# From block 1 to block 2 of a three-block transformer on one core: the two norms made row block by row block, and their preparations moved

## Chip, cores and metric

One Trainium2 chip, one of its cores. The metric is the time of one execution on the device, in microseconds (us); the kernel is one launch. Engines are named as in the profile: PE (TensorE, with PEld for its weight loads), DVE (VectorE), ACT (ScalarE), POOL (GpSimd) and SP (SyncE, which here issues transfers).

## What is computed

Three different transformer blocks, one after the other, on one sequence of 512 tokens of width 1024, all in float32. Cut to what matters:

```
x = first_block(x, c, ...)     # retention, dilated attention, then 32 experts, top 4; ends with a norm
x = second_block(x, ...)       # begins with a norm, then projections, attention, pooling, feed-forward
return third_block(x, ...)

def rms_norm(x, g):
    return x * rsqrt(mean(x * x) + EPS) * g
# at the turn: x = rms_norm(x, g_final); h = rms_norm(x, attn_norm_g_2); u = h @ w_in_2
```

So at the turn from block 1 to block 2 there are two norms in a row: the first gives the residual stream of block 2, the second, of that, gives the input of its projections. With s the sum of squares of x and s' that of x times the gain, both roots follow from the two sums alone: the second norm's sum is s' + EPS (s + D EPS), up to the factor 1/D.

## The kernel before, in words

Tokens are held as NT = 4 tiles of P = 128 rows; the features are D = 1024, or KD = 8 groups of 128 when turned. Weights come as chunks of 1 MB through a ring of six slots (`RING`), which SP fills in a fixed order; each consumer counts a chunk as used (`chunk_used`), and SP then loads the one six places on. A stage is a `Block`: a piece of program for each engine, with all engines meeting at its end. A function scope (`Kit.scope`, one for each block of the model) ends with another such meeting, in which SP clears semaphores.

**Precise products.** A float32 weight piece is split in two: ACT rounds it (`make_high`, L312) and POOL subtracts (`make_low`, L317). A chunk is split in two halves, places 0 and 1, in the tile `split_w`. The activations are split the same way, in `pair`. A product is three matmuls: high by high, low by high, high by low. `SplitAhead` is what one stage does for the first chunk of the next: `high_ahead` and `low_ahead` make place 0. `Onward` goes further: it makes place 1 too (`high`, `low`) and multiplies place 0 (`products`, L363) before the stage ends, so that the next stage begins with place 1 (L661 in `linear_split`) while ACT and POOL make the next piece.

**The experts' stage** (`mixture`) runs 34 units of work in a loop whose order is written out by hand: ACT rounds (L2149), DVE subtracts (L2159), PE multiplies (L2399 with the high, L2403 with the low part), POOL gathers rows and adds results into memory by indirect transfers (L2310). The low parts live in two buffers, `moe_low0` (two of six halves) and `moe_low1` (four), which is allocated in `mixture`. When the last unit's results are in memory, SP loads the four tiles of x back (L2521), each with its own semaphore `x_arrived[t]`.

**The turn** (`leave_and_enter`, one Block) is where the change is:

- SP issues the loads of columns, of the lambda vectors and of the modulation bias, then makes the tables of relative bias: a row out to memory (L1577, when DVE has copied it), spread (L1580), back in as tables (L1585); `bias.sp_end` waits until these are there.
- ACT issues a few loads (`bias.sp_load`, `C.sp`), rounds place 1 of the next chunk (`onward.high`), loads the square-root table by a one-column root (`act_root_table`, L158), then squares x and x times gain for each tile with the sum in an accumulator (L1231, L1234), takes all roots in one instruction (L1237), makes the sigmoid of the condition vector (`M.act_begin`, L989), the exponential of lambda (`lam.act`, L1637), shares the evacuation of the turned tiles (`N.act_evac`: L910, L926) and makes two tiles of the residual (L1245).
- DVE multiplies the four tiles by the gain (L1254), copies the bias row (L1603) and the columns (L770), does the first lambda operations (`lam.dve_begin`, L1630 to L1633), closes the sums of all tiles at once (L1260, L1263), inverts (L1266), scales the four tiles (L1270), shares the evacuation (`N.dve_evac`: L950, L933), makes the other two residual tiles (L1273), then the condition vector (`M.dve_begin`: L999, L1003) and the last of lambda (`lam.dve_end`: L1642, L1643).
- PE makes the bias row (L1598) and turns the columns (L766), waits for all four tiles (`N.pe_turn`: 32 transposes, group by group of features, L904), then does `onward.products`.
- POOL does only `onward.low`.

The next stage is `linear_split` for `b2_qkv` (L661, then L674), then `rest_projections` (L459), then `diff_attention`, which is the first to read the bias tables.

## Time and profile before

| | |
|---|---|
| three runs, median (lowest to highest) | 3656.51 us (3655.53 to 3659.17) |
| the profiled execution, its own time | 3660.48 us |
| its span | 3658.7 us |
| mean granted clock of TensorE | 0.961 |
| PE busy | 3401.1 us (93%) |
| PEld busy | 2758.6 us (75%) |
| DVE busy | 2094.0 us (57%) |
| ACT busy | 1762.2 us (48%) |
| POOL busy | 1036.4 us (28%) |
| HBM read | 669.00 MB |

The span is cut by the page in 40 slices of 91 us; in the slices of the experts PE and DVE are both at nine tenths or more, and the turn falls in the one after, where PE is at six tenths. Shares of the whole span say little of a turn of some 40 us; it is read from the timeline, from the waits and from windows. A timeline row gives the start, the time taken (of several instructions together where it says xN), the engine, the line, output and input, and in brackets how long the engine was idle before and what ended that. PEq, ACTq and SPq are the queues of an engine. In windows the columns are busy time and count of PE, PEld, DVE, ACT and POOL, then the granted clock as a share of full speed, the busy share of the transfer engines and GB/s.

### The profile page before, as it was taken

The page shows a single profiled execution, that of the slowest core. Times are in us where ns is not written, and L with a number is a line of the kernel's source. Part 1 is how long each engine was busy: PE and PEld are TensorE (multiplying, and loading weights), DVE is VectorE, ACT ScalarE, POOL GpSimd, SP SyncE. Part 2 cuts the span into 40 slices and gives each one's busy share as a digit, 9 for nine tenths or more (in the row PEclk, how much of TensorE's full clock was granted, in tenths as well). Part 3 has the DMA queues.
Part 4 walks back from the last instruction along what each step waited for, and adds up shares of the span by engine and source line. Part 5 has one row for each costly group of instructions (what it writes and reads, how often), then busy time and mean ns, then how long its engine had stood idle before and what let it go on. Part 6 is the DMA issues. An engine that isn't in the chain of part 4 may idle for free. (4 is left out here: it accounts for less than half of the span.)

```text
span 3658.7 us, 55859 instructions
## 1 busy us (share of the span) xinstructions
PE 3401.1 (93%) x20953; PEld 2758.6 (75%) x20953; DVE 2094.0 (57%) x2485; ACT 1762.2 (48%) x2315; POOL 1036.4 (28%) x435
## 2 busy tenths in 40 slices
PE   7989999989999999999999697899999987789997
PEld 4877777668888888888888583678887866678886
DVE  3320121279999999999999426411142155346665
ACT  3222333257777777777777424322233243133333
POOL 2334222212232323232323230134443300034443
PEclk9999999989999999999999899799999988889999
DMA  8213343359999999999999527023232210012321
GB/s 285 77 61 102 119 129 121 112 215 371 378 369 377 368 380 366 382 365 378 367 383 365 184 89 294 21 84 104 87 98 70 93 31 4 7 59 94 102 93 40
DMA packets 245517, 696.92 MB, mean 190 GB/s; under 512 B 17878, under 2 KB 149834, under 8 KB 186748
## 3 DMA queue, kind: packets, MB, share of 16 engines
q1 hardware_dynamic: 235196, 658.52, 48.5%
q0 software_dynamic: 9936, 36.18, 3.8%
q8 instruction: 111, 1.82, 0.2%
q14 instruction: 34, 0.28, 0.0%
q10 hardware_dynamic: 240, 0.12, 0.0%
HBM read 669.00 MB, written 30.23 MB: 191 GB/s over the span
## 5 line engine op out<-in xcount | busy, mean ns | idle before, releaser
L317 POOL TENSOR_TENSOR split_w<-ring,split_w 128x1024 fp32r<-128x1024 f32 (+1 forms) x294 | 698.5, 2376 | 1647.3 <-ACT split_w L312 1468.3
L2159 DVE TENSOR_TENSOR moe_low<-ring,moe_high 128x2048 fp32r<-128x2048 f32 x408 | 929.0, 2284 | 18.4 <-ACT moe_high L2149 17.4
L2149 ACT ACTIVATE moe_high<-ring 128x1024 fp32r<-128x1024 f32 x810 | 827.5, 1058 | 102.9 <-PE psum L2403 102.4
L312 ACT ACTIVATE split_w<-ring 128x1024 fp32r<-128x1024 f32 (+1 forms) x294 | 304.5, 1036 | 1034.5 <-PE psum L488 608.1
L2399 PE MATMUL psum<-moe_high,moe_xe 128*128 128x512 f32 x2176 | 585.3, 391 | 0.0
L2399 PEld LDWEIGHTS psum<-moe_high,moe_xe 128*128 128x128 f32 x2176 | 410.0, 188 | 84.0
L2310 POOL DMA_INDIRECT moe_y_rows<-moe_ye,moe_target x34 | 197.4, 5807 | 696.3 <-DVE moe_ye L2214 696.3
L488 PE MATMUL psum<-pair,split_w 128*128 128x512 f32 x1488 | 339.5, 390 | 4.3 <-PEq L3755 4.3
L2403 PE MATMUL psum<-moe_low,moe_xe 128*128 128x512 f32 x1088 | 336.3, 390 | 0.0
L488 PEld LDWEIGHTS psum<-pair,split_w 128*128 128x128 f32 x1488 | 280.4, 189 | 62.8 <-POOL split_w L317 4.4
L488 PE MATMUL psum<-b_pair,split_w 128*128 128x512 f32 x1392 | 321.9, 392 | 5.8 <-PEq L1388 2.6
L488 PEld LDWEIGHTS psum<-b_pair,split_w 128*128 128x128 f32 x1392 | 262.2, 189 | 63.2 <-issue 8.8
L2399 PE MATMUL psum<-moe_high,moe_aT 128*128 128x512 f32 x1088 | 301.9, 399 | 0.0
L2403 PEld LDWEIGHTS psum<-moe_low,moe_xe 128*128 128x128 f32 x1088 | 204.5, 188 | 43.3
L488 PE MATMUL psum<-b_hpair,split_w 128*128 128x512 f32 x1008 | 228.6, 389 | 0.0
L2399 PEld LDWEIGHTS psum<-moe_high,moe_aT 128*128 128x128 f32 x1088 | 196.8, 188 | 36.3
L488 PEld LDWEIGHTS psum<-b_hpair,split_w 128*128 128x128 f32 x1008 | 189.2, 188 | 39.3
L2403 PE MATMUL psum<-moe_low,moe_aT 128*128 128x512 f32 x544 | 168.0, 390 | 0.0
L674 PE MATMUL psum<-split_w,b_hpair 128*128 128x512 f32 x672 | 156.8, 395 | 7.3 <-DVE b_hpair L565 7.1
L674 PEld LDWEIGHTS psum<-split_w,b_hpair 128*128 128x128 f32 x672 | 127.9, 191 | 35.9 <-issue 9.2
L459 PE MATMUL psum<-split_w,b_pair 128*128 128x256 f32 x1152 | 144.6, 288 | 4.1 <-PEq L727 2.2
L459 PEld LDWEIGHTS psum<-split_w,b_pair 128*128 128x128 f32 x1152 | 142.0, 196 | 7.3 <-issue 4.5
(636 smaller groups left out, 4361.7 us busy)
## 6 DMA issues: line engine op xcount, KB each, us to landing
ring<-in_w_experts SPq DMA_DIRECT2D x408, 1024.0 KB, 8.1
ring<-in_w_mod SPq DMA_DIRECT2D x48, 1024.0 KB, 6.1
ring<-in_w_in SPq DMA_DIRECT2D x39, 1024.0 KB, 5.3
ring<-in_w_up SPq DMA_DIRECT2D x33, 1024.0 KB, 5.1
ring<-in_w_in SPq DMA_DIRECT2D x44, 512.0 KB, 5.2
ring<-in_w_down SPq DMA_DIRECT2D x20, 1024.0 KB, 5.1
ring<-in_w_gate SPq DMA_DIRECT2D x11, 1024.0 KB, 5.3
ring<-in_w_out SPq DMA_DIRECT2D x8, 1024.0 KB, 6.2
```

Of the source, the lines that this page charges most:

```text
L312: self.nc.scalar.activation(high, raw, ACT.Copy).then_inc(self.K.rounded, 1)
L317: self.nc.gpsimd.tensor_tensor(low, raw, high.bitcast(F32), ALU.subtract).then_inc(self.K.split, 1)
L459: ins = self.nc.tensor.matmul(out, x(a, r0 + k), w[:, b, k, :], start=(opens and r0 + k + a + b == 0), stop=(closes and r0 + k == KD - 1 a ...
L488: ins = self.nc.tensor.matmul(out[:, tile, :], w[:, a, k, cols], pair[:, b, r0 + k, :], start=(r0 + k + a + b == 0), stop=(r0 + k == nk - ...
L674: ins = nc.tensor.matmul(out[:, t, 0:width], x[:, a, k, t * P:(t + 1) * P], w[:, b, k, :], start=(r + k + a + b == 0), stop=(r + k == tota ...
L2149: self.nc.scalar.activation(self.B["high"][:, j % HALVES, :], self.raw(j), ACT.Copy).then_inc(self.high, 1)
L2159: self.nc.vector.tensor_tensor(flat(self.low_of(j, 2)), self.K.ring[:, self.ring_slot(j // 2), :], high, ALU.subtract).then_inc(self.low, 2)
L2310: self.nc.gpsimd.indirect_dma_start(self.B["y_rows"], bass.IndirectOffsetOnAxis(ap=self.B["target"][:, 0:1], axis=0), self.B["ye"][:, :], ...
L2399: nc.tensor.matmul(out, lhs[:, part, k0 + k, :], high[:, k, :], start=(k0 + k + part == 0 and not started), stop=False)
L2403: ins = nc.tensor.matmul(out, lhs[:, 0, k0 + k, :], low[:, k, :], start=False, stop=(k0 + k == KD - 1))
```

## The change

At the end of the experts' stage ACT and POOL now make both halves of the next chunk (`high_whole`, `low_whole`), and ACT then takes a one-column root into a new tile `moe_root`, allocated ahead of `moe_low1`. In the turn `onward.high`, `onward.low` and `act_root_table` are gone. Sums, roots, inversions and scalings are done tile by tile. The exponential of lambda and the first lambda operations come after the residual tiles. The transposes are done tile by tile, with matmuls whose results nobody reads (`idle`) ahead of them: 12 of 384 columns ahead of the first tile, eight of 128 columns ahead of each later one, into a bank that is overwritten later. The wait for the bias tables goes from the turn to the start of SP's part of `rest_projections`.

```diff
--- before.py
+++ after.py
@@ -179,6 +179,12 @@
                 sp.wait_ge(self.chunk_used, n + 1)
                 self.issue(sp, n + RING)
 
+    def idle(self, count, out):
+
+        n = out.shape[-1]
+        for _ in range(count):
+            self.nc.tensor.matmul(out, self.w[:, 1, 0, 0:P], self.w[:, 1, 1, 0:n], start=True, stop=True)
+
     def wait_chunk(self, pe, n):
         pe.wait_ge(self.landed[n % RING], self.stream.landed_at[n])
 
@@ -323,6 +329,15 @@
     def low_ahead(self, po):
         if self.next is not None:
             self.make_low(po, self.next, 0)
+
+    def high_whole(self, sc):
+
+        self.make_high(sc, self.next, 0)
+        self.make_high(sc, self.next, 1)
+
+    def low_whole(self, po):
+        self.make_low(po, self.next, 0)
+        self.make_low(po, self.next, 1)
 
 
 class Onward(SplitAhead):
@@ -1197,8 +1212,8 @@
 
     nc = K.nc
     n_ = lambda s: K.sem(f"turnover_{s}")
-    first, scaled, second, summed, root, inverted = (
-        n_(s) for s in ("first", "scaled", "second", "summed", "root", "inverted"))
+    first, scaled, second, summed, total, root, inverted = (
+        n_(s) for s in ("first", "scaled", "second", "summed", "total", "root", "inverted"))
     with ExitStack() as ctx:
         N = Norm(K, "b2_norm", ctx, C.cols[:, C.at[key]:C.at[key] + KD], None, dst, pair, xg)
         onward = Onward(K, "b2_qkv", "N", pair, N)
@@ -1212,18 +1227,16 @@
                 lam.sp(sp)
                 M.sp_bias(sp)
                 bias.sp_spread(sp)
-                bias.sp_end(sp)
-
-            @block.gpsimd
-            def _(po):
-                onward.low(po, 0)
 
             @block.scalar
             def _(sc):
                 bias.sp_load(sc)
                 C.sp(sc)
-                onward.high(sc)
-                K.act_root_table(sd[:, 0, :])
+
+                def roots(t):
+                    sc.wait_ge(total, t + 1)
+                    nc.scalar.activation(sd[:, :, t], sums[:, :, t], ACT.Sqrt, scale=1.0 / D).then_inc(root, 1)
+
                 for t in range(NT):
                     sc.wait_ge(K.x_arrived[t], 16)
                     if t == 3:
@@ -1233,19 +1246,35 @@
                     sc.wait_ge(scaled, t + 1)
                     nc.scalar.activation(junk(t), xg[:, t, :], ACT.Square, accum_out=sums[:, 1, t:t + 1])\
                         .then_inc(second, 1)
-                sc.wait_ge(summed, 2)
-                nc.scalar.activation(sd[:, :, :], sums[:, :, :], ACT.Sqrt, scale=1.0 / D).then_inc(root, 1)
+                    if t:
+                        roots(t - 1)
+                roots(NT - 1)
                 sc.wait_ge(C3.copied, 1)
                 M.act_begin(sc)
-                lam.act(sc)
-                sc.wait_ge(inverted, 1)
                 sc.wait_ge(C.copied, 1)
                 N.act_evac(sc)
+                sc.wait_ge(inverted, NT)
                 for t in (0, 1):
                     nc.scalar.activation(K.x[:, t, :], xg[:, t, :], ACT.Copy, scale=r[:, 0, t:t + 1])
+                lam.act(sc)
 
             @block.vector
             def _(ve):
+                def totals(t):
+                    ve.wait_ge(first, t + 1)
+                    nc.vector.tensor_scalar(sums[:, 0, t:t + 1], sums[:, 0, t:t + 1], D * EPS, None, ALU.add)\
+                        .then_inc(summed, 1)
+                    ve.wait_ge(second, t + 1)
+                    ve.wait_ge(summed, t + 1)
+                    nc.vector.scalar_tensor_tensor(sums[:, 1, t:t + 1], sums[:, 0, t:t + 1], EPS, sums[:, 1, t:t + 1],
+                                                   ALU.mult, ALU.add).then_inc(total, 1)
+
+                def normalise(t):
+                    ve.wait_ge(root, t + 1)
+                    nc.vector.reciprocal(r[:, :, t], sd[:, :, t]).then_inc(inverted, 1)
+                    ve.wait_ge(inverted, t + 1)
+                    nc.vector.tensor_scalar(tile(t), xg[:, t, :], r[:, 1, t:t + 1], None, ALU.mult).then_inc(N.normed, 1)
+
                 M.dve_constants(ve)
                 bias.dve_begin(ve)
                 ve.wait_ge(K.gain_loaded, 16)
@@ -1253,24 +1282,18 @@
                     ve.wait_ge(K.x_arrived[t], 16)
                     nc.vector.tensor_tensor(xg[:, t, :], K.x[:, t, :], K.gain, ALU.mult).then_inc(scaled, 1)
                 bias.dve_rows(ve)
+                ve.wait_ge(scaled, NT)
+                totals(0)
                 C.ve(ve, 0)
                 C3.ve(ve, 1)
-                lam.dve_begin(ve)
-                ve.wait_ge(first, NT)
-                nc.vector.tensor_scalar(sums[:, 0, :], sums[:, 0, :], D * EPS, None, ALU.add).then_inc(summed, 1)
-                ve.wait_ge(second, NT)
-                ve.wait_ge(summed, 1)
-                nc.vector.scalar_tensor_tensor(sums[:, 1, :], sums[:, 0, :], EPS, sums[:, 1, :], ALU.mult, ALU.add)\
-                    .then_inc(summed, 1)
-                ve.wait_ge(root, 1)
-                nc.vector.reciprocal(r[:, :, :], sd[:, :, :]).then_inc(inverted, 1)
-                ve.wait_ge(inverted, 1)
-                ve.wait_ge(scaled, NT)
-                for t in range(NT):
-                    nc.vector.tensor_scalar(tile(t), xg[:, t, :], r[:, 1, t:t + 1], None, ALU.mult).then_inc(N.normed, 1)
+                for t in range(1, NT):
+                    totals(t)
+                    normalise(t - 1)
+                normalise(NT - 1)
                 N.dve_evac(ve)
                 for t in (2, 3):
                     nc.vector.tensor_scalar(K.x[:, t, :], xg[:, t, :], r[:, 0, t:t + 1], None, ALU.mult)
+                lam.dve_begin(ve)
                 M.dve_begin(ve)
                 lam.dve_end(ve)
 
@@ -1282,7 +1305,16 @@
                 pe.wait_ge(C.copied, 1)
                 pe.wait_ge(C3.copied, 1)
                 pe.wait_ge(bias.copied, 1)
-                N.pe_turn(pe)
+                K.idle(12, K.ps[:, 7, P:])
+                for t in range(NT):
+                    if t:
+                        K.idle(8, K.ps[:, 7, 3 * P:])
+                    pe.wait_ge(N.normed, t + 1)
+                    for k in range(KD):
+                        ins = nc.tensor.transpose(K.ps[:, k, t * P:(t + 1) * P], tile(t)[:, k * P:(k + 1) * P],
+                                                  K.ident[:, :])
+                        if t == NT - 1:
+                            ins.then_inc(N.turned, 1)
                 onward.products(pe)
 
 
@@ -2484,6 +2516,7 @@
     assert last - first == RING and 12 % RING == 0 and PER % HALVES == 0 and PER % 6 == 0
     after, B, X, y_started, y_complete = SplitAhead(K, last), mix.B, mix.X, mix.y_started, K.sem("moe_y_complete")
     with ExitStack() as ctx:
+        root = K.sb(ctx, "moe_root", [P, 1])
         B["low1"] = K.sb(ctx, "moe_low1", [P, HALVES - 2, HALF], F32R)
         with nc.Block() as block:
             @block.sync
@@ -2546,7 +2579,7 @@
                 with po.Fori(0, n1) as u:
                     X.pool_unit(po, u)
                 X.pool_unit(po, n1, ahead=False)
-                after.low_ahead(po)
+                after.low_whole(po)
 
             @block.scalar
             def _(sc):
@@ -2558,7 +2591,8 @@
                 with sc.Fori(0, n1) as u:
                     X.act_unit(sc, u)
                 X.act_unit(sc, n1, ahead=False)
-                after.high_ahead(sc)
+                after.high_whole(sc)
+                K.act_root_table(root)
 
             @block.tensor
             def _(pe):
@@ -2931,7 +2965,7 @@
         K.load(sp, self.sg[:, :], A["da_subln_g_2"][0].rearrange("(p a) -> p a", a=1))
 
 
-def rest_projections(K, pair, rest, glrT, qk, qkT, gq):
+def rest_projections(K, pair, rest, glrT, qk, qkT, gq, bias):
 
 
     nc, ps = K.nc, K.ps
@@ -2949,6 +2983,7 @@
         with nc.Block() as block:
             @block.sync
             def _(sp):
+                bias.sp_end(sp)
                 K.refill(sp, first, end)
 
             @block.gpsimd
@@ -3319,7 +3354,7 @@
                 linear_split(K, "b2_qkv", "N", pair, 2,
                              act=lambda j, b: nc.scalar.activation(dests[j], b, ACT.Copy))
                 qkT = K.hT[:, :, :].rearrange("p (a h) n -> p a h n", a=2)
-                rest_projections(K, pair, rest, glrT, qk, qkT, lam.gq[:, 0:1])
+                rest_projections(K, pair, rest, glrT, qk, qkT, lam.gq[:, 0:1], bias)
             G = TailConstants(K, right)
             diff_attention(K, "da", qkT[:, 0, :, :], qkT[:, 1, :, :], v, TB, lam.neg[:, :], qk[:, 0, :, :], ss, M, G)
             da.close()
```

## Rows read from the trace of the kernel before

**Rows 1.** Waits of TensorE, 2000 to 2100: total us, times, longest
```profile
PE psum L904 <- DVE b_rest L1270: 10.1, 1, 10.1
```

**Rows 2.** Timeline, all engines: start, us, engine, what, idle before
```profile
2026.36 1.06 ACT L312 ACTIVATE split_w<-ring 128x1024 fp32r<-128x1024 f32 x1
...
2035.49 2.92 POOL L317 TENSOR_TENSOR split_w<-ring,split_w 128x1024 fp32r<-128x1024 f32 x1
...
2040.63 1.77 SPq L2521 DMA_DIRECT2D x_res<-moe_y_rows  x4
...
2046.95 1.06 ACT L312 ACTIVATE split_w<-ring 128x1024 fp32r<-128x1024 f32 x1 [19.53 <-issue]
...
2048.02 1.28 ACT L158 ACT_TABLE_LOAD   x1
...
2048.09 2.62 POOL L317 TENSOR_TENSOR split_w<-ring,split_w 128x1024 fp32r<-128x1024 f32 x1 [9.67 <-ACT split_w L312]
...
2049.20 2.29 PE L1598 MATMUL psum<-b_rest,b_bias_rel 33*4 33x512 f32 x4 [16.32 <-DMA b_rest<-in_k_hot]
...
2049.55 1.06 ACT L1231 ACTIVATE hT<-x_res 128x1024 f32<-128x1024 f32 x1
...
2057.39 1.06 ACT L1234 ACTIVATE hT<-b_qk 128x1024 f32<-128x1024 f32 x1
```

**Rows 3.** The same timeline, VectorE
```profile
2052.85 0.80 DVE L1603 COPY b_rest<-psum 4x640 f32<-4x640 f32 x1
...
2056.83 0.29 DVE L1633 TENSOR_REDUCE b_ls<-b_lp 128x2 f32<-128x128 f32 x1
...
2058.57 0.16 DVE L1263 SCALAR_TENSOR_TENSOR turnover_sums<-turnover_sums 128x4 f32<-128x4 f32 x1 [1.01 <-ACT hT L1234]
...
2059.01 0.20 DVE L1266 RECIPROCAL turnover_r<-turnover_sd 128x8 f32<-128x8 f32 x1 [0.28 <-ACT turnover_sd L1237]
...
2060.58 1.41 DVE L1270 TENSOR_SCALAR b_rest<-b_qk,turnover_r 128x1024 f32<-128x1024 f32 x2
```

**Rows 4.** The same timeline, from the transposes to the next stage
```profile
2062.14 0.66 PE L904 MATMUL psum<-identity,b_v 128*128 128x128 f32 x2 [10.07 <-DVE b_rest L1270]
...
2063.34 0.69 ACT L910 ACTIVATE hT<-psum,b_cols 128x512 f32<-128x512 f32 x1 [1.33 <-PE psum L904]
...
2071.59 2.18 ACT L1245 ACTIVATE x_res<-b_qk,turnover_r 128x1024 f32<-128x1024 f32 x2
...
2072.33 1.41 DVE L1273 TENSOR_SCALAR x_res<-b_qk,turnover_r 128x1024 f32<-128x1024 f32 x2
...
2074.24 0.15 DVE L1643 TENSOR_SCALAR b_neg_lam<-b_neg_lam 128x1 f32<-128x1 f32 x1
...
2074.92 5.72 PE L661 MATMUL psum<-split_w,b_pair 128*128 128x512 f32 x24 [1.21 <-PEq L1208]
```

**Rows 5.** Line L1254 in two stretches: ns min/median/max, first and last start
```profile
L1254 DVE TENSOR_TENSOR b_qk<-x_res,hT x2: 1218/1222/1225, 2046.1 to 2047.3; 128x1024 f32<-128x1024 f32 x2
...
L1254 DVE TENSOR_TENSOR b_qk<-x_res,hT x2: 1218/2293/3368, 2047.3 to 2048.4; 128x1024 f32<-128x1024 f32 x2
```

**Rows 6.** Windows: busy and count of each engine, clock, DMA
```profile
2062.20:2067.00 4.80, 4.80 (x23) 4.80 (x24) 2.79 (x5) 3.21 (x6) 0.00 (x0) 0.50 0.56 174
2067.10:2068.00 0.90, 0.90 (x11) 0.90 (x9) 0.80 (x2) 0.90 (x2) 0.00 (x0) 1.00 0.84 264
2138.90:2142.10 3.20, 3.20 (x17) 3.20 (x16) 3.15 (x2) 0.00 (x0) 1.92 (x1) 0.50 0.08 31
2142.30:2145.00 2.70, 2.70 (x25) 2.70 (x24) 2.57 (x4) 0.16 (x1) 0.00 (x0) 1.00 0.03 6
```

**Rows 7.** Timeline, TensorE, where block 2's later projections begin
```profile
2137.26 2.94 PE L459 MATMUL psum<-split_w,b_pair 128*128 128x256 f32 x18 [2.22 <-PEq L727]
```

**Rows 8.** Lines L2403 and L2206: ns min/median/max
```profile
L2403 PE MATMUL psum<-moe_low,moe_xe x1088: 387/389/628, 791.8 to 2019.7; 128*128 128x512 f32 x182
...
L2206 DVE TENSOR_TENSOR moe_xe<-psum,moe_xe x34: 1216/1218/1225, 788.2 to 1994.6; 128x1024 fp32r<-128x1024 f32 x34
```

## The prediction

> **What bounds the kernel now.** The waits of TensorE are read first, between the last expert and the projections of block 2: the longest with a computing engine behind it is 10.1 us, in front of the transposes of L904, until VectorE has made the last normalised tile (L1270) [rows 1]. The timeline then gives the chain that leads there. The residual stream is loaded back by SyncE at 2040.63 (L2521), which nothing in the change touches. ScalarE issues its own small loads, makes the second half of the next weight piece at 2046.95 (L312, 1.06 us), loads the square-root table at 2048.02 (1.28 us) and only then squares, from 2049.55; eight squares later the last pass of L1234 begins at 2057.39 [rows 2]. VectorE closes the sums at 2058.57, inverts at 2059.01, and the last pair of tiles starts at 2060.58 and takes 1.41 us, so all four tiles are there at 2061.99 [rows 3]. The first evacuation is at 2063.34, ScalarE goes on to the residual tiles at 2071.59, VectorE at 2072.33, its last small operation ends at 2074.24 + 0.15 = 2074.39, and the next stage's matmuls start at 2074.92 [rows 4]. The stage is this chain; after it TensorE runs without a pause for some 60 us. So only what moves 2074.92 counts.
>
> **The squares start earlier.** The second half (L312) and the root table move into the experts' stage. There ScalarE is free from 2026.36 + 1.06, GpSimd ends its one piece at 2035.49 + 2.92 = 2038.4, and a second of 2.6 us ends at 2041.0, before SyncE's four loads of 2040.63 + 1.77 are issued [rows 2]. Cost there: nothing; if that cover were gone, each microsecond past 2042.4 would go on the chain. In the next stage the squares start at about 2046.95 in place of 2049.55, 2.6 us earlier.
> VectorE gains too. Three multiplications of L1254 take 1.22 us, but the one begun at 2048.4 takes 3.37 [rows 5], while GpSimd splits the second half at 2048.09 for 2.62 us [rows 2]. With that piece gone the four end near 2046.14 + 4 x 1.17 = 2050.8, in place of 2052.9.
>
> **Block row by block row.** The bias matmuls end at 2049.20 + 2.29 = 2051.5 [rows 2], and VectorE copies their row (0.80 us, L1603) [rows 3] before it closes the first sums. That is 2052.3, and with two small operations 2052.7. ScalarE has squared two tiles by 2046.95 + 2 x 2.2 = 2051.4 (a pair takes (2057.39 + 1.06 - 2049.55)/4 = 2.2) and waits 1.3 us in its first root. Queued behind that root are the squares of tiles 2 and 3 and the later roots: 2053.0, 2055.2, 2055.4, 2057.6. VectorE finishes two tiles of 0.7 us and two inversions of 0.2 after that: the fourth tile at 2059.8, 2.2 us before today's 2061.99. Two column copies follow the first sums, so the columns and the bias row are there at 2053.1; that releases TensorE.
>
> **The padding matmuls.** Unlike today's, TensorE's queue now holds work of its own: 12 matmuls of 384 columns, then eight transposes a tile with eight matmuls of 128 columns ahead of each later tile. The windows give the prices. At the 1.2 GHz level a transpose is 4.8/23 = 0.21 us and a 256-column matmul 3.2/17 = 0.19; at 2.4 GHz a transpose is about 0.9/9 = 0.10 (by its nine weight loads) and a 256-column matmul 2.7/25 = 0.11 [rows 6]. So 384 columns at the low level are 0.3 us, the twelve 3.6, from 2053.1 to 2056.7. The clock rose 5.0 us after the transposes began (2062.1 [rows 4] to 2067.1 [rows 6]); I put the rise at 2058.1. The first tile's transposes then end at 2058.3. A 128-column matmul has no row: between half of the 256-column one (0.054) and the whole of it (0.108). I take 0.054, as it is the same operation on the same weights at half the length: 0.43 for eight. Three such groups and two more tiles (0.84 each) put the last tile's transposes at 2058.3 + 1.3 + 1.7 = 2061.3, later than its data (2059.8). The padding, and not the norm, is then what is late; at 0.108 it is 2062.6.
> Today the first evacuation follows the first transpose by 1.2 us, of which four transposes at the low level are 0.84. Now one is enough: 2061.3 + 0.1 + 0.36 = 2061.8, in place of 2063.34. **Gain 1.5 us** (upper bound 3.1, with the padding free; lower bound 0.2).
>
> **The tail.** From the first evacuation to VectorE's residual tiles are 9.0 us, to ScalarE's 8.25 [rows 4]; both keep their pace. Today the stage ends 2074.92 - 2063.34 = 11.6 us after the first evacuation. Now the exponential of lambda comes after ScalarE's residual tiles (2.18 us), so its table load lies bare: 8.25 + 2.18 + 1.28 + 0.2 = 11.9. VectorE has 9.0 + 1.41, then the three lambda operations (0.8 with the 0.29 of L1633, [rows 3]) and the two for the condition vector, 11.6, and waits for it; two small operations (0.3) and the turn of the stage (0.53) give 12.8. **Loss 1.2 us** (0.4 to 2.0: below if the lambda operations overlap, above if the table is loaded only when the sums are there).
> About the table the trace is plain: from the end of L312 at 2048.01 to the first square at 2049.55 there are 1.54 us, which hold the load of 1.28 and the one-column root, and nothing else [rows 2]. The Trainium skill, ScalarE: Activation LUTs, section What ACT_TABLE_LOAD costs, adds a drain of some 1380 ns to each switch; by it the sum below would be 1.4 us more.
>
> **SyncE.** The wait for the bias tables goes to the projections after. Today SyncE is through before VectorE, whose end sets the turn of the stage, so nothing is gained; where the wait now stands it delays the first refill only if the table has not landed by some 2075, and the ring is full then. Cost nothing.
>
> **Sum.** -1.5 + 1.2 = -0.3 us. The profiled execution took 3660.48, with a span of 3658.7, and would come to 3660.2; it lies 4.0 above the median of the three runs shown, 3656.51, so the median comes to 3656.2. Measurement tells 0.2% (7.3 us) from no change; even the full 3.1 us of the earlier norm would be 0.08%.
>
> **Rivals.** First, **the dear end of the tail**. VectorE and ScalarE hold the stage while TensorE is through with its 24 products at 2061.8 + 4.9 + 5.7 = 2072.4, 2.3 us before the next. In front of L459 it stood idle for 2.22 us [rows 7], and the window behind it ran at 0.50 from 2138.9 to 2142.1 [rows 6], which costs half of that, 1.6 us. With it, padding at 0.108 and the late table: -0.3 + 1.6 + 1.3 + 0.8 = +3.4, 3659.9. Against: idle for 1.2 us cost none today. Chance 0.2.
> Second, **the norm's gain comes whole**: padding at its cheapest with an early rise of the clock, evacuation from 2060.3, tail 12.8: -1.8, 3654.7. Against it stands the count of matmuls in the queue. Chance 0.1.
> Third, **the bare table load waits for ScalarE's pipeline to empty**, behind residual tiles, where at 2048 it did not wait: at most one such tile, 2.18/2 = 1.1 us [rows 4], so +0.8, 3657.3. Chance 0.05, since at 2048 there is no room for it. That is the drain of the Trainium skill's ScalarE page; its own figure would give 3657.6.
> Fourth, **the experts' stage slows down**. The new one-column tile is allocated ahead of the low weights' second buffer and moves its start by 32 bytes; that buffer holds four of six parts of what L2159 writes and L2403 reads. L2403 has the 1088 matmuls of its row and half as many in the second product [rows 8], so 1088 of the 1632 read it. It decides from 7.3/1088 = 7 ns on a matmul of 5.72/24 = 0.238 us (L661, [rows 4]), 3%. At 5% it would be 13 us: 3669.5. Against it: VectorE writes 1024 columns in 1218 ns into a tile at a multiple of 64 bytes (L2206, [rows 8]) and in 1222 into one that is 32 off (L1254, [rows 5]); no row shows a fast matmul with such an operand. Chance 0.1. The same shift with the other sign, or the later stages' clock falling better, is what is left for faster: 0.05.
> That the change doesn't do what it says: were the root table loaded again in the new stage, 1.3 us of ScalarE's wait for the first sums would hide it. It changes no number.
>
> **Numbers.** The likeliest is the sum (0.5), with 3654 to 3659. Sum and first three rivals, 0.85, are all within 0.2%; slower 0.10, faster 0.05. The range goes from 3652.5 (the second rival, less the 1 us by which runs lie under their median and one for the clock) to 3663.0 (the first, plus the 2.7 by which a run lay above).
>
> **What would show it.** In the changed trace: no L312 and no table load at the stage's start, first square near 2047 if the stage starts at 2044.9; four multiplications of 1.2 us; ScalarE idle some 1.3 us in the first root; the fourth tile of L1270's kind 2 us earlier, but its transposes waiting behind padding and not behind it; a table load after ScalarE's residual tiles, and VectorE waiting for its exponential; 2033 to the next stage's matmul 42 us as today, give or take 2. Experts' L2403 at 389 ns as before. The prediction is wrong if those two move, if that stretch shrinks by over 3 us, or if the clock falls in the stage after.

## The result, and the profile after

| | before | after |
|---|---|---|
| median, runs beside each other | 3659.1 us (8 runs, 3652.7 to 3663.8) | 3672.2 us (8 runs, 3665.8 to 3676.0) |
| profiled execution, span | 3660.48, 3658.7 | 3671.52, 3669.7 |

The ratio is 1.0039, with an interval of 1.0030 to 1.0048: slower by 14 us, where 3656.2 and no difference had been forecast. The fourth rival's price of 3669.5 is the nearest, but its mechanism turns out to be less than half of the loss.

Cutting both traces at the same events gives the account of the 11.0 us between the two spans:

| stretch, us | before | after | difference |
|---|---|---|---|
| start of the span to the first expert matmul | 789.7 | 790.8 | +1.1 |
| first to last expert matmul | 1243.2 | 1249.0 | **+5.8** |
| last expert matmul to SyncE's load of x | 7.75 | 7.75 | 0.0 |
| that load to the turn's first VectorE operation | 4.29 | 6.58 | **+2.3** |
| turn: start to first evacuation | 18.42 | 16.49 | -1.9 |
| turn: first evacuation to the next stage's matmul | 11.58 | 12.60 | +1.0 |
| everything behind it | 1583.75 | 1586.43 | **+2.7** |

The turn itself is 0.9 us shorter. All of the loss lies outside the stretch that the sum had been made for. The first row is no part of the argument: over all seventeen profiles of this case that stretch varies by 3.6 us, with nothing changed in it.

**The experts' matmuls.** The line's durations (ns, min/median/max) in the profile after, to be read beside [rows 8], where the median is 389:

```profile
L2435 PE MATMUL psum<-moe_low,moe_xe x1088: 387/393/628, 792.9 to 2026.6; 128*128 128x512 f32 x182
L2435 PE MATMUL psum<-moe_low,moe_aT x544: 387/395/401, 817.9 to 2039.5; 128*128 128x512 f32 x182
```

The lines by form (busy us, mean ns), before and then after, say the same in sums. The low products grow by 3.9 and 2.6 us:

```profile
L2403 PE MATMUL psum<-moe_low,moe_xe 128*128 128x512 f32 x1088 | 336.3, 390 | 0.0
L2403 PE MATMUL psum<-moe_low,moe_aT 128*128 128x512 f32 x544 | 168.0, 390 | 0.0
```

```profile
L2435 PE MATMUL psum<-moe_low,moe_xe 128*128 128x512 f32 x1088 | 340.2, 394 | 0.0
L2435 PE MATMUL psum<-moe_low,moe_aT 128*128 128x512 f32 x544 | 170.6, 395 | 0.0
```

**The way into the turn.** The timeline of the same stretch as [rows 2]; first before, then after:

```profile
2034.46 1.58 POOL L2310 DMA_INDIRECT moe_y_rows<-moe_ye,moe_target  x1 [18.45 <-DVE moe_ye L2214]
...
2044.92 0.17 DVE L993 MEMSET mod_heads<- 128x128 f32 x1 [11.25 <-PEq L130]
```

```profile
2041.43 1.58 POOL L2342 DMA_INDIRECT moe_y_rows<-moe_ye,moe_target  x1 [16.00 <-DVE moe_ye L2246]
2042.46 5.21 POOL L323 TENSOR_TENSOR split_w<-ring,split_w 128x1024 fp32r<-128x1024 f32 x2
2047.60 1.77 SPq L2554 DMA_DIRECT2D x_res<-moe_y_rows  x4
...
2054.18 0.17 DVE L1008 MEMSET mod_heads<- 128x128 f32 x1 [13.54 <-PEq L130]
...
2055.40 4.63 DVE L1283 TENSOR_TENSOR b_qk<-x_res,hT 128x1024 f32<-128x1024 f32 x4
...
2056.14 1.06 ACT L1244 ACTIVATE hT<-x_res 128x1024 f32<-128x1024 f32 x1 [19.39 <-issue]
```

GpSimd's last subtraction ends at 2035.49 + 2.92 = 2038.41 before and the turn starts 6.51 us later; after, it ends at 2042.46 + 5.21 = 2047.67 and the turn starts 6.51 us later. SyncE's issue ends 2.52 us ahead of the turn before and 4.81 after. The constant is GpSimd's: in all fifteen profiles in which GpSimd subtracts at the end of that stage it is 6.51 or 6.52 us. The four multiplications of L1283 take 4.63 us together, as predicted. The Trainium skill, SBUF — State Buffer, section SBUF: two separate sides, says that a VectorE operation with two SBUF inputs and a GpSimd operation that reads SBUF exclude one another for a whole instruction. The trace agrees: the one of 3.37 us in [rows 5] is gone now that GpSimd is idle, and in three kernels below in which GpSimd's piece is back in the turn the four take 6.79 us together.

**The turn.** The timeline after, from the bias matmuls to the next stage:

```profile
2056.75 2.29 PE L1630 MATMUL psum<-b_rest,b_bias_rel 33*4 33x512 f32 x4 [16.90 <-DMA b_rest<-in_k_hot]
...
2061.12 0.21 ACT L1238 ACTIVATE turnover_sd<-turnover_sums 128x2 f32<-128x2 f32 x1 [0.43 <-DVE turnover_sums L1269]
...
2061.44 3.80 PE L186 MATMUL psum<-split_w 128*128 128x384 f32 x12 [1.08 <-DVE b_cols L785]
...
2065.87 1.09 PE L186 MATMUL psum<-split_w 128*128 128x128 f32 x8
...
2067.05 0.75 DVE L1276 TENSOR_SCALAR b_rest<-b_qk,turnover_r 128x1024 f32<-128x1024 f32 x1
...
2070.28 1.06 PE L1314 MATMUL psum<-identity,b_rest 128*128 128x128 f32 x8
2070.67 0.69 ACT L925 ACTIVATE hT<-psum,b_cols 128x512 f32<-128x512 f32 x1 [2.86 <-PE psum L1314]
...
2073.49 7.31 PE L378 MATMUL psum<-split_w,b_pair 128*128 128x512 f32 x24 [2.15 <-DVE b_pair L948]
...
2080.87 1.28 ACT L1669 ACT_TABLE_LOAD   x1
2082.16 0.20 ACT L1669 ACTIVATE b_ls<-b_ls 128x2 f32<-128x2 f32 x1
2082.40 0.16 DVE L1674 TENSOR_TENSOR b_neg_lam<-b_ls 128x1 f32<-128x1 f32 x1 [0.46 <-ACT b_ls L1669]
...
2083.27 2.97 PE L676 MATMUL psum<-split_w,b_pair 128*128 128x512 f32 x12 [2.47 <-PEq L1223]
```

Two of its windows (columns as in [rows 6]):

```profile
2061.40:2065.00 3.60, 3.56 (x12) 3.59 (x13) 2.22 (x8) 3.54 (x8) 0.00 (x0) 0.55 0.43 126
2065.00:2071.40 6.40, 6.34 (x58) 6.07 (x56) 2.52 (x6) 3.35 (x8) 0.00 (x0) 1.00 0.66 200
```

The fourth tile is there at 2067.8 and its transposes begin at 2070.28: for 2.5 us TensorE is behind with padding, as the prediction had it. The bias matmuls wait for a small table (`in_k_hot`) that ScalarE's queue loads at the start of the turn. They begin 2.57 us after that start; in the kernel before it was 4.28.

### The profile page after: what moved, and what is told of

Its sections match the earlier page's. It is cut to its first block and busy times, and to the rows that moved or that the text cites. A ratio compares the mean times of both kernels' runs of the same rounds, so it can differ in the third digit from the quotient of the medians.

```text
span 3669.7 us, 55945 instructions
## 1 busy us (share of the span) xinstructions
PE 3418.2 (93%) x20989; PEld 2761.1 (75%) x20989; DVE 2093.1 (57%) x2494; ACT 1764.4 (48%) x2318; POOL 1045.3 (28%) x435
```

## The experiments

Each time stands beside runs of the kernel before on the same chip: 3655.8 us for the first four kernels below; 3657.9 for SyncE's wait, the two parts and the third kernel without padding; 3658.7 for the norm's part with both kinds of padding and the three on lambda; 3653.6 for the padding alone, the first twelve and the second profile of the norm's part with padding. So ratios can be compared across the groups, and times only within one. The intervals reach 3 to 4 us to each side, and 4 to 5 where a kernel has only six runs. Every variant computes the whole result; the padding matmuls compute nothing that is read.

**The new tile alone.**

```diff
+        root = K.sb(ctx, "moe_root", [P, 1])
         B["low1"] = K.sb(ctx, "moe_low1", [P, HALVES - 2, HALF], F32R)
```

> The kernel before with one thing of the change: the one-column tile, allocated ahead of the second buffer of the experts' low weights and used by nothing. Theory A (the shift of that buffer slows the matmuls that stream from it): in the changed kernel's trace the second of the two low matmuls of a product follows the first by 236 ns where the buffer is the shifted one and by 227 where it is not; so here the same, the mean of the low matmuls at 394 to 395 ns in place of 390, the stretch from the first to the last expert matmul 1248.6 us in place of 1242.8, and the time 6 us (0.16%) above the kernel before. Theory B (the experts' stage of the changed kernel is slower for another reason, such as the code behind its loop): 1242.8 us and no difference.

3663.3 us, ratio 1.0016 (1.0007 to 1.0025). As Theory A has it: the first to the last expert matmul takes 1249.5 us, and the durations are those of the kernel after:

```profile
L2403 PE MATMUL psum<-moe_low,moe_xe x1088: 387/393/632, 793.6 to 2027.7; 128*128 128x512 f32 x182
L2403 PE MATMUL psum<-moe_low,moe_aT x544: 387/395/401, 818.9 to 2040.5; 128*128 128x512 f32 x182
```

**The change with the tile behind the buffer.**

```diff
-        root = K.sb(ctx, "moe_root", [P, 1])
         B["low1"] = K.sb(ctx, "moe_low1", [P, HALVES - 2, HALF], F32R)
+        root = K.sb(ctx, "moe_root", [P, 1])
```

> The changed kernel with the one-column tile allocated behind the second buffer of the low weights, so that the buffer starts where it did before. Theory A (address): the experts' stretch goes back to 1242.8 us and the time falls by 6 us against the changed kernel, to 0.15 to 0.25% above the kernel before (what is left is the later start of the turn, 2.3 us, the rest unexplained). Theory B: the stretch stays at 1248.6. Both: from SyncE's loads of x to the first operation of the turn 6.5 us, as in the changed kernel (4.2 before).

The stretch is back at 1243.1 us and the line at its old durations:

```profile
L2435 PE MATMUL psum<-moe_low,moe_xe x1088: 387/389/628, 791.7 to 2019.5; 128*128 128x512 f32 x182
```

The time stays at 3671.0, ratio 1.0034 (1.0022 to 1.0047). In this execution everything behind the turn took 1591.6 us instead of 1583.75. So the 6 us of the tile are shown by the stretch, here and in the kernel with the tile alone; the time of this one does not show them, since its interval overlaps that of the kernel after. The kernel has further losses, and they vary more from run to run.

**The second subtraction on VectorE** (on top of the last), then both.

```diff
 def low_whole(self, po):
     self.make_low(po, self.next, 0)
-    self.make_low(po, self.next, 1)
...
                 X.dve_unit(ve, n1, ahead=False)
+                after.dve_low(ve)
```

> As the kernel with the tile behind, and the second half of the next weight piece is subtracted by VectorE at the end of the experts' stage in place of GpSimd. Theory C (the turn starts late because GpSimd reaches the end of the stage a fixed time, some 5.7 us, after its last subtraction, and has one more now): the turn starts 2.3 us earlier against the experts' last matmul than in the changed kernel, 4.2 us after SyncE's loads as before. Theory D (ScalarE's extra piece and root table, or something else, hold the end of the stage): 6.5 us stays.

> As the kernel with the tile behind, with both halves subtracted by VectorE, GpSimd having nothing behind the last scatter. Theory C: GpSimd no longer holds the end of the stage, SyncE does, so the turn starts 2.1 to 2.6 us after SyncE's first load of x is issued (1.77 us of issuing and the meeting), 1.6 to 2 us earlier than in the kernel before. Rival: GpSimd's end waits for the scatter itself and not for the subtractions, and the turn starts 4.2 us after the loads, or later. Time in the first case at or below the kernel before (-0.05 to +0.1%).

With one: 3664.8, ratio 1.0021 (1.0012 to 1.0030); with both: 3664.3, 1.0020 (1.0011 to 1.0030). The turn starts 4.27 and 3.61 us after the load of x. The timelines, with one and with both:

```profile
2036.99 2.92 POOL L323 TENSOR_TENSOR split_w<-ring,split_w 128x1024 fp32r<-128x1024 f32 x1
2042.15 1.77 SPq L2559 DMA_DIRECT2D x_res<-moe_y_rows  x4
2046.42 0.17 DVE L1013 MEMSET mod_heads<- 128x128 f32 x1 [10.33 <-PEq L130]
```

```profile
2033.51 2.35 DVE L345 TENSOR_TENSOR split_w<-ring,split_w 128x1024 fp32r<-128x1024 f32 x2
2034.39 1.79 POOL L2347 DMA_INDIRECT moe_y_rows<-moe_ye,moe_target  x1 [15.91 <-DVE moe_ye L2251]
2040.53 1.77 SPq L2559 DMA_DIRECT2D x_res<-moe_y_rows  x4
2044.14 0.17 DVE L1013 MEMSET mod_heads<- 128x128 f32 x1 [8.28 <-PEq L130]
```

With one, 2036.99 + 2.92 + 6.51 = 2046.42, where the turn does start. With both, GpSimd has no subtraction and the turn starts 1.84 us after SyncE's issue: now SyncE holds it. That is 0.7 us earlier than before, not the 2 expected; the least distance to SyncE is 1.84. The 2.3 us by which the turn starts late are shown, and that the turn before is held by GpSimd too. The 0.7 us bring nothing: the first evacuation comes 21.7 us after the load of x in both kernels. The bias matmuls, which wait for their table, begin 8.5 and 8.3 us after that load. Both kernels keep a loss of 7 us, and in both the window behind the turn now opens at half clock: the stage of the projections takes 64.9 and 65.0 us instead of 62.3.

**SyncE's wait alone, the two parts alone, and the padding.**

```diff
 def rest_projections(K, pair, rest, glrT, qk, qkT, gq, bias):
             def _(sp):
+                bias.sp_end(sp)
                 K.refill(sp, first, end)
```

> The kernel before with only SyncE's wait for the bias tables moved from the turn to the projections after. The kernels with the buffer back in its place and the late start of the turn taken away still took 7 to 8 us more than the kernel before, where the stretches up to the next stage add up to 0.4 us. Theory R1 (the moved wait holds a refill): that loss shows here, +7 us (0.2%). Theories R2 to R4 (padding, norm part, experts' part): no difference, within 0.05%.

3658.6 us, ratio 1.0002 (0.9994 to 1.0011): no cost that can be seen, as predicted.

The experts' part alone, with the tile behind and the second subtraction on VectorE (cut: in the turn the rounding, the subtraction and the root table are gone, as in the change):

```diff
-                after.high_ahead(sc)
+                after.high_whole(sc)
+                K.act_root_table(root)
...
                 X.dve_unit(ve, n1, ahead=False)
+                after.dve_low(ve)
```

> The kernel before with only the part in the experts' stage: both halves rounded there, the second subtracted by VectorE, the root table loaded there, the new tile behind the low weights. The norms are made whole, as before. Theory R4 (this part costs later): +7 us less the 1.5 to 2.5 us by which the squares and with them the stage are earlier. Other theories: the turn's first evacuation 16 us after its start in place of 18.4, the next stage 2.3 us earlier, time 2 us (0.06%) below the kernel before.

3654.5 us, ratio 0.9997 (0.9988 to 1.0005). The first evacuation comes 17.2 us after the turn's start, 1.2 sooner (the expectation had 16); nothing is lost, so Theory R4 fails.

The third kernel of this group without its padding, and the norm's part alone, also without:

```diff
-                K.idle(12, K.ps[:, 7, P:])
                 for t in range(NT):
-                    if t:
-                        K.idle(8, K.ps[:, 7, 3 * P:])
                     pe.wait_ge(N.normed, t + 1)
```

> The kernel with the tile behind and the second half subtracted by VectorE, without the matmuls whose results nobody reads. The transposes then wait for their tiles. Theory R2 (the padding costs later, through the clock or the power of what follows): the time falls by 7 us to that of the kernel before. Other theories: it stays 7 to 8 us above, less 1 to 2 us because the first evacuation comes earlier (the last tile is there 2 to 3 us before its transposes in the padded kernel; against it 8 transposes at 1.2 GHz in place of 2.4).

> The kernel before with only the turn's norms made row block by row block and lambda's operations at the end of the stage, without padding; both halves, the root table and SyncE's wait as before. Theory R3 (the tail of the stage leaves TensorE idle 2.3 us or more, and the clock falls in the next stage, and more behind it): the next stage's 24 first products begin 12.6 us after the first evacuation in place of 11.6, the stage behind it takes 64 to 65 us in place of 62.3, and the time is 3 to 8 us above the kernel before. Otherwise within 1 us of it.

3660.7, ratio 1.0005 (0.9995 to 1.0014), and 3660.2, 1.0006 (0.9997 to 1.0015). Without padding the first evacuation comes 15.63 us after the turn's start, against 17.45 with it. So the idle matmuls cost 1.8 us on the chain and some 6 us in the time, as Theory R2 has it. The norm's part alone shows the mechanism of Theory R3 but not its price: the tail is 12.60 us, TensorE idle for 4.07 of them, and the projections take 65.1, yet the time is 2.2 us above the kernel before and not 3 to 8, which these runs can't tell from nothing.

Then the padding was added to what had been free of it:

> The kernel before with the norm part (row block by row block, lambda at the end) and the padding matmuls, here from the place-0 half; no part of the experts' stage. Theory P (the padding matmuls cost time behind the turn, by how the clock of TensorE falls and rises in later stages): the time is 3 to 6 us above the norm part alone, 5 to 8 above the kernel before, with the added time in the profile's stages of block 3 (the causal attention at 89 us, not 85.4). Theory Q (the remainder comes of the experts' part and the norm part together): within 2 us of the norm part alone; the first evacuation 1 to 2 us later than there.

> Edit: the kernel before, with 36 padding matmuls of 384 columns (nothing reads their result) put on TensorE's queue ahead of its wait for the four normalised tiles, and nothing else. They cost 3.6 us for twelve at the low level by the prediction's price, some 8 to 11 us in all, inside the 10.1 us in which TensorE waits there today, so the padding itself is hidden but for at most 2 us. Theory P (padding makes TensorE warm ahead of the turn and the time comes back behind it, in later stages at the low clock): the turn gets shorter by some 2 us, since all transposes run at the full clock, and yet the time rises by 3 to 10 us, to 3661 to 3669. Theory N (padding as such is harmless, and the loss in the kernels with it comes from the per-tile order together with it): 3655 to 3660.

> Edit: z3_norm_padding without the three groups of eight 128-column padding matmuls between the tiles; the twelve of 384 columns stay. Theory P1 (it is the early warm clock that counts, which the twelve alone bring): as z3, 3668 to 3673. Theory P2 (it is the padding between the tiles that holds the transposes up and lets the clock go on high): as y4 without padding, 3659 to 3663.

```diff
+                K.idle(36, K.ps[:, 7, P:])
                 N.pe_turn(pe)
```

(this one is the padding alone, in the kernel before)

| kernel | time | kernel before, beside it | ratio |
|---|---|---|---|
| norm's part | 3660.2 | 3657.9 | 1.0006 (0.9997 to 1.0015) |
| with both kinds of padding | 3671.7 | 3658.7 | 1.0034 (1.0022 to 1.0046) |
| with the first twelve only | 3660.6 | 3653.6 | 1.0017 (1.0007 to 1.0026) |
| kernel before with 36 matmuls of padding | 3664.9 | 3653.6 | 1.0024 (1.0014 to 1.0034) |

Both kinds of padding cost 10 us against the norm's part alone, more than Theory P asked; the first evacuation comes 19.73 us after the turn's start, against 17.27. The first twelve alone cost some 4 us, which lies between Theories P1 and P2. Its 3660.6 us is a number of P2, but it stands beside runs that are 4 to 5 us faster than those the theories were priced on, and its interval overlaps those of both neighbours: the two are not told apart. They leave the chain as it was (17.31 us).

Padding alone, with no other edit, costs 0.24%, some 9 us, although its turn is 0.7 us shorter (2 expected): Theory P, not N. The windows of that kernel (busy us and count of PE, PEld, DVE, ACT, POOL, then clock, DMA share, GB/s) show what it does do, during it, behind it and in the transposes:

```profile
2054.90:2057.70 2.80, 2.80 (x9) 2.80 (x10) 0.43 (x2) 2.77 (x6) 0.00 (x0) 0.50 0.61 192
2057.70:2062.70 5.00, 5.00 (x29) 4.68 (x27) 3.42 (x9) 4.68 (x9) 0.00 (x0) 1.00 0.58 180
2062.90:2066.50 3.60, 3.57 (x32) 3.48 (x32) 2.16 (x4) 2.73 (x5) 0.00 (x0) 1.00 0.83 273
```

It raises the clock before the transposes. What follows, stage by stage, in the kernel before and in this one (the projections, the stages up to block 3's attention, that attention, its scan, the rest):

```profile
2074.80:2137.20 62.40, 60.12 (x264) 49.47 (x264) 0.00 (x0) 17.08 (x14) 26.37 (x11) 1.00 0.25 73
2137.20:2974.10 836.90, 771.58 (x3806) 611.67 (x3806) 268.19 (x348) 276.17 (x429) 261.77 (x110) 0.94 0.31 103
2974.10:3063.90 89.80, 75.96 (x432) 61.53 (x432) 63.48 (x133) 37.88 (x93) 0.00 (x0) 0.84 0.01 2
3063.90:3192.60 128.70, 95.43 (x5152) 86.63 (x5152) 40.04 (x58) 17.78 (x31) 0.00 (x0) 0.83 0.02 5
3192.60:3658.70 466.10, 430.47 (x1866) 352.79 (x1866) 277.85 (x278) 168.80 (x201) 183.50 (x75) 0.96 0.23 77
```

```profile
2074.90:2138.80 63.90, 61.60 (x264) 50.55 (x264) 0.00 (x0) 17.07 (x14) 26.37 (x11) 0.97 0.25 71
2138.80:2975.00 836.20, 770.98 (x3806) 611.88 (x3806) 268.13 (x348) 276.34 (x429) 261.91 (x110) 0.94 0.31 103
2975.00:3064.20 89.20, 75.45 (x432) 60.96 (x432) 63.44 (x133) 37.96 (x93) 0.00 (x0) 0.83 0.01 2
3064.20:3197.60 133.40, 96.72 (x5152) 86.62 (x5152) 40.05 (x58) 17.81 (x31) 0.00 (x0) 0.82 0.02 5
3197.60:3660.60 463.00, 427.02 (x1866) 349.51 (x1866) 278.03 (x278) 168.80 (x201) 183.23 (x75) 0.97 0.23 77
```

Same matmuls, same counts; single stages differ by 0.6 to 4.7 us, in either direction. Together it is 1.8 us more in this pair, in which the execution before lies above its kernel's median and the other below. The attention stage shows how little one execution says here. The norm's part without padding has 85.4 us where these, one of them without padding as well, have 89.8 and 89.2, at another clock:

```profile
2976.90:3062.30 85.40, 71.59 (x432) 57.11 (x432) 63.45 (x133) 37.77 (x93) 0.00 (x0) 0.88 0.01 2
```

The norm's part with padding has a second profile, since the first execution (3663.0 us) was a short one:

> The same kernel as z3_norm_padding, for a second profile, since that one's profiled execution was the shortest of its six (3663.0 beside a median of 3671.7). Theory P: an execution near 3671 shows its additional 8 us behind the turn, in block 3's attention and scan stages, at the low clock (89 to 90 us and 135 to 137 us, in place of 86.3 and 133.5). Theory E (it comes from ahead of the turn, the start of the kernel or the experts' stage): those two as in z3, and the stretch up to the experts or the experts' 1243.4 longer by 8 us.

It took 3664.9 and is a partial answer: behind the turn it took 1585.7 us instead of 1584.3, with 89.0 instead of 86.3 in block 3's attention and 133.5 in both in the scan. The stretch up to the experts and theirs differ by 0.3 us. No execution near 3671 of this kernel was profiled.

Where the loss lies follows better from times and traces together. From the first expert matmul to the first matmul of the next stage a trace gives each kernel's difference to the kernel before. Taken from the difference that the ratio gives, it leaves what must lie behind the turn. Left are 6.5 to 9.9 us in the eight kernels with padding (7.0 in the kernel after, 9.6 with the padding alone, 6.5 with the first twelve only) and -0.5 to 3.0 us in the seven others. Each value is uncertain by the interval of its ratio, but those of the two groups do not overlap. So the place of the loss is behind the turn.

Single profiles point the same way, though weakly. Everything behind the turn took 1576.8 to 1585.9 us in the eight profiles without padding (mean 1582.1) and 1584.3 to 1591.6 in nine with it (mean 1588.0). But three of those without, all from one chip, are the three shortest; without that chip's four the mean is 1584.8. What the length does follow, over all seventeen, is the time for which the granted clock is at its low level there: 1576.8 us with 198.7 of them low (SyncE's wait alone), 1583.8 with 212.6 (before), 1591.6 with 233.0 (tile behind), a correlation of 0.89. The low time itself overlaps: 198.7 to 219.4 us without padding, 201.9 to 233.0 with it. Why padding would change what stages 900 us on are granted was not settled, and stays open.

**The exponential of lambda moved ahead of the evacuation.** It takes the bare table load off the tail, and VectorE's first lambda operations move ahead of its evacuation with it; without padding, with VectorE making both subtractions as well, and with padding:

```diff
                 M.act_begin(sc)
+                lam.act(sc)
                 sc.wait_ge(C.copied, 1)
...
                     nc.scalar.activation(K.x[:, t, :], xg[:, t, :], ACT.Copy, scale=r[:, 0, t:t + 1])
-                lam.act(sc)
...
                 normalise(NT - 1)
+                lam.dve_begin(ve)
                 N.dve_evac(ve)
...
-                lam.dve_begin(ve)
                 M.dve_begin(ve)
```

> The kernel without padding (tile behind, second half by VectorE), and lambda's first operations and exponential made where ScalarE waits for the transposes, ahead of the evacuation. Theory T (the bare table load at the end costs 1.0 us, and the longer idle of TensorE makes the clock fall in the next stage, 1.6 to 2.8 us more): from the first evacuation to the next stage 11.6 us in place of 12.6, the stage behind it 62.3 us in place of 63.9 to 65.1, and the time 2 to 4 us below the kernel without padding, so 0 to 0.1% below the kernel before. Against it: if the exponential delays the evacuation, that begins up to 0.5 us later and the 1.0 us shrinks.

> The same, with both halves subtracted by VectorE, so that GpSimd has nothing behind the last scatter. The turn starts 0.7 us earlier against SyncE's loads (3.6 in place of 4.3); 0.7 us less time than the kernel with lambda early at best. If the first evacuation waits for something that does not move (the small tables' loads), nothing.

> The padded kernel (tile behind, second half by VectorE) with lambda early. Theory T: 11.6 in place of 12.6 us from the first evacuation on, the stage behind it 62.3 in place of 64.9, together 3.6 us less than the padded kernel, 3 us above the kernel before. Theory P alone: 1 us less, and 5 to 6 above the kernel before, since what the padding costs behind the turn stays.

3660.0, ratio 0.9997 (0.9988 to 1.0006); 3659.6, 0.9999 (0.9991 to 1.0008); 3665.9, 1.0017 (1.0008 to 1.0027). The tail falls from 12.60 to 11.33 or 11.35 us in all three, and start to next matmul is 27.2 us in the first against 30.0 before. There the projections take 62.3 us, as Theory T has it; in the other two TensorE still stands idle for 2.81 us in front of them, and they take 63.9. The padded kernel gains 1.5 us by its ratio, not the 3.6 of Theory T: what the padding costs stays, as Theory P alone had it. The earlier start of the turn in the second is again lost: its bias matmuls begin 9.3 us after the load of x and its first evacuation comes after 20.9, against 8.5 and 20.1 in the first.

The whole does not become faster by what the turn gives: the best version of the change equals the kernel before. None beats it by more than its interval.

## Why the prediction was wrong

The sum was made for the turn alone, and three terms outside it stood at nothing. Those are the steps that failed: the experts' stage as it was (+5.8 us), "Cost there: nothing" for the second piece at its end (the turn starts 2.3 us late), and padding that costs only in TensorE's queue (some 7 us more behind the turn). The first two are shown, each with its place, by edits of their own. Of the third, the largest, the cost is shown and its path is not. The first stood as the fourth rival at 0.1; the third was in no case, so that the total came near that rival's 3669.5 is chance.

- **The experts' stage.** The likeliest case had it unchanged; the fourth rival, at 0.1, was what happened. Its place (four of six parts, read by 1088 matmuls) was right, and its size was 4% of one of the two matmuls that read a piece. Priced at 5%, it gave 13 us (3669.5 leaves out the -0.3 of the sum); measured, 5.8 to 6.3. What was taken against it, that VectorE writes as fast into a tile 32 bytes off [rows 5, 8], says nothing of TensorE's reading. It was a row of another engine. With no row for the operand, both outcomes should have stood near even.
- **"Cost there: nothing"** was wrong. It compared the end of GpSimd's work with SyncE's issue, and took it as covered until 2042.4. What held the stage's end was GpSimd itself, 6.51 us behind its last subtraction. That could be read from the trace of before: 2038.41 to 2044.92, with SyncE done at 2042.40. A second piece of 2.3 to 2.6 us then goes wholly onto the turn's start: +2.3 us. The second bound on the step was missing. (Some of it comes back in the turn, as said next.)
- **The turn.** Right in direction, and near in size in part by luck. The first evacuation is 1.9 us sooner after the turn's start (1.5 predicted; the last tile 2.5 us ahead of its transposes). The tail grew by 1.0 (1.2 predicted), 12.60 against 12.8. The term of 0.054 us for a padding matmul of 128 columns was mis-sized: from the first of eight to the transposes behind them (2065.87 to 2066.80) are 0.93 us, 0.12 each, over the upper end of 0.108. Two things made that good. The clock rose sooner: the window of the first padding matmuls has 0.55, a tenth of it at the high level, and the one behind it 1.00, so it rose some 3.2 us after the first of them, not 5.0. And the bias matmuls began 2.57 us after the turn's start, not 4.28, so ScalarE waited 0.43 us in its first root, not 1.3, and the padding began 7.3 us after the start, not 8.2. In all seventeen profiles they begin 8.3 to 9.3 us after SyncE's load of x is issued, wherever the turn starts: the late start hides part of itself. Counted from that load the first evacuation is at 22.7 us before and 23.1 after; with the start back in its place (the third kernel of the experiments) it is at 21.7, a gain of 1.0.
- **The table.** It cost 1.28 us and a start at 2082.16, 1.29 after it began at 2080.87. No drain, in the place where it had been feared. The 1.38 us of the Trainium skill, ScalarE: Activation LUTs, section What ACT_TABLE_LOAD costs, are not to be seen here either; the measurement decides.
- **The clock behind the turn.** In the kernel after, TensorE stood idle for 2.47 us in front of the next stage (2.3 in the first rival), and the projections did not slow: 62.3 us. In eleven other profiles it stood for 2.5 to 4.1 us, and they took 63.8 to 65.1, 1.4 to 2.8 more; in the five, the kernel before among them, where it stood for 1.3 at most, 62.3: the first rival's mechanism, at about its price of 1.6. Why the kernel after escaped it is not shown. The one without padding has the same idle time, 2.49 us, and its 24 products ran partly at the low level as well (7.29 us and 7.31, against 5.71 before), and it did slow, to 63.9.
- **What was not in any case**: that padding costs in later stages. It was costed on its own queue only, and the comparisons of times give it 6 to 10 us where all of it is there. In three such pairs 1.7 to 2.5 us of that lie in the turn; with the padding alone the turn is 0.7 us shorter, and the loss is there all the same. Nothing in the prediction asked what it changes in later stages.
- **SyncE's wait**: right, and tested alone.
- **The signs.** One of the prediction's own signs told of the tile: L2403 was not at 389 ns as before, its median is 393. The stretch from 2033 to the next stage, 42.0 us before and 43.4 after, stayed within its 2 us and so hid the late start.

The sum of the shown parts against the 14 us: 5.8 (tile) + 2.3 (GpSimd) - 0.9 (turn) = 7.2 us. Some 7 us are left, give or take 3, and the comparisons of times put them on the padding; by which path is open. The pair of profiles alone shows only 2.7 of them.

## What to carry to other kernels

A small allocation ahead of a matmul operand moves its start: put new tiles behind the buffers that TensorE reads at full rate (shown here for one buffer), and compare one line's median duration before anything else. When work is put at the end of a stage, ask of each engine when it arrives, not when its last instruction ends; GpSimd's arrival was 6.5 us after. Then ask what else the next stage waits for: a start 0.7 us earlier brought nothing here, where the stage's first matmuls wait for a small table. Matmuls that fill idle time are not free even where they hide, and a chain shortened by 3 us near the middle of the program may give nothing at its end, so measure the whole.

## What the runs showed of the hardware that was not expected

- Where a moving operand starts 32 bytes off a multiple of 64, the second of two matmuls of 512 columns starts 236 ns after the first; where it starts on the multiple, 227 (the same buffer, with and without a tile of 32 bytes ahead of it). No other offset and no other operand was tried.
- From the end of GpSimd's last subtraction to the next stage's first operation there are 6.51 or 6.52 us in fifteen profiles; from the end of SyncE's last issue the least was 1.84.
- 36 hidden matmuls whose result nobody reads cost 0.24% of the whole (0.14 to 0.34%), behind the stage that they are in.
- Behind the turn an execution is on the whole the longer, the longer its clock is granted at the low level: from 1576.8 us with 198.7 of them low to 1591.6 with 233.0, a correlation of 0.89 over seventeen profiles.
